# Output projection and feed-forward of the first 384 tokens moved between the recurrence stages of blocks 3 to 7

## The chip, the core and the metric

The kernel runs on one core of a Trainium2 chip. Its time is device microseconds from launch to end, the median of three runs. The engines are TensorE (PE), VectorE (DVE), ScalarE (ACT), GpSimd (POOL) and SyncE (SP, which here only issues the weight loads). Each has its own queue, executed in order; they meet through semaphores.

## What is computed

One step of a hybrid decoder layer, for 1024 prompt tokens and 8 sample tokens (1032 columns, kept with features on the partitions), model width 1024:

```python
h = rmsnorm(x, g_norm1) * (1 + sc1) + sh1
mix, states = token_mix(h, ...)       # h @ w_in, then HGRN2 | Mamba-2 | RWKV-7, then @ w_out
x = x + g1 * mix
h = rmsnorm(x, g_norm2) * (1 + sc2) + sh2
ff = (silu(h @ w_gate) * (h @ w_up)) @ w_down      # D_FF = 2816
x = x + g2 * ff
y = rmsnorm(x, g_final)
```

`sh1` to `g2` come from a modulation matmul of the conditioning vectors with `w_ada`. The recurrences carry a state over the tokens, so a token's mixed row needs all tokens before it; projection and feed-forward are independent from token to token.

## The kernel before

**Dense matmuls.** A dense product is cut into units (128 output features) and each unit into quanta, one for each chunk of 344 columns (`CH`, three chunks). In a quantum, `dense(q)` runs over the 128-row tiles k of the contraction: every fp32 product is made of three matmuls, hi by hi, lo by hi, hi by lo (lines 1067 to 1069). A unit's weights are loaded once by SP into one of three buffers (`RAW`, line 759), cast to `WHI` by ACT (`split_hi`, line 1547), and `WLO`, the remainder, is subtracted by DVE (`split_lo`, line 1944) or POOL (`split_rest`, line 846). Each quantum fills one PSUM bank, which ACT or DVE takes up (`bring_out`). The next quantum in that bank waits for that.

**Phases.** All engines follow written-out lists, with a barrier (`end_phase`) between them. PLAN1 holds the input projection, the last part of it in gaps of the WKV recurrence. PLAN2 holds the HGRN2 and Mamba-2 recurrences in eight blocks of 128 tokens. A block is the sequence hg_att, hg_state, mb_decay, hg_o, hg_logits, mb_prod, hg_sq, hg_gate, mb_turn, mb_sq, hg_out, hg_levels, mb_out, hg_x, where logits, gate, turn and levels are those of the next block. The main chain is: PE turns and attention matmuls (1015, 1348), state (1355), decay sums (1406), DVE's segments (2548), ACT's exponential (1851), DVE's product MM (2553), PE's products (1417, 1418, states 1421), then DVE's output and square (HT, 2504), the norms (1374, 1431), and for the next block DVE's differences and levels (2453 to 2470). hg_x turns one block of input tokens into `XT`, the residual. Sixteen quanta of the modulation matmul (`ada`, 1074) are dealt out, one each after mb_decay, mb_prod and mb_turn; each reads two `RAW` buffers. At the end of PLAN2 stand the samples' one-token updates (`smp_tok`, `smp_state`, `smp_out`; DVE lines 2587 to 2606), which pass through DRAM.

**PLAN3** is the rest: the mixed rows are split in hi and lo (`mixsplit`), then `out`, then the norm for each chunk (`sum`, `scaled`, `rest`: sum over partitions on PE at 1090, DVE, ACT at 1621, DVE), then gate and up (interleaved by chunk), with SiLU on ACT and the product on DVE, and `down` in four groups of 6, 6, 5 and 5 tiles, the last norm (`normed`), and nine turned output tiles (`y`) of which two buffers (`OT`) are written to DRAM in turn.

Of the kernel before, what the change touches and what calls it, by code (L numbers as in the profile page):

```python
# [33 lines left out]
F32 = mybir.dt.float32  # L34
# [19 lines left out]
GROUPS = [6, 6, 5, 5]  # L54
MAXG = max(GROUPS)
# [63 lines left out]
def dense_plan():  # L119
# [7 lines left out]
    units += [('out', t) for t in range(8)]  # L127
    f = 0
    for g, n in enumerate(GROUPS):
        for i in range(n):  # L130
            units += [('gate', f), ('up', f)]
            f += 1
        units += [('down', (g, d)) for d in range(KT)]
    return units, n1


def kernel_program(nc, ins, outs):
# [15 lines left out]
    UNITS, N1 = dense_plan()  # L153
    QUANTA, FIRSTQ, LASTQ = [], {}, {}
    u = 0
    while u < len(UNITS):
# [9 lines left out]
        elif kind == 'gate' or UNITS[u] in (('out', KT - 2), ('down', (len(GROUPS) - 1, KT - 2))):  # L166

            FIRSTQ[u + 1] = len(QUANTA) + 1
            for c in range(NCH):
                QUANTA += [(u, c), (u + 1, c)]  # L170
            LASTQ[u] = len(QUANTA) - 2
            LASTQ[u + 1] = len(QUANTA) - 1
            u += 2
            continue
        else:
            QUANTA += [(u, c) for c in range(NCH)]
# [5 lines left out]
    QP2 = LASTQ[N1 - 1] + 1  # L182
    NRAW, NSPL1, NSPL3 = 3, 2, 4
# [26 lines left out]
    SQUARED = [q for q, (u, _) in enumerate(QUANTA)  # L210
               if UNITS[u][0] == 'out' or (UNITS[u][0] == 'down' and UNITS[u][1][0] == len(GROUPS) - 1)]
    TILE_IN_GROUP = [i for n in GROUPS for i in range(n)]

    ctx = ExitStack()
    with ctx:
# [131 lines left out]
        HB2 = [r2.t(f"HB{i}", [P, 6, BLK]) for i in range(2)]  # L347
# [6 lines left out]
        HD = r2.t("HD", [P, 6, 2, BLK])  # L354
# [7 lines left out]
        HVD = r2.t("HVD", [P, 2, 4, BLK])  # L362
        HSH = r2.t("HSH", [P, 5, 2, 64])
        HO = r2.t("HO", [P, 2, BLK])
        HT = r2.t("HT", [P, 2, BLK])
        HR = r2.t("HR", [P, 2, BLK])
        XD = r2.t("XD", [P, 8, 64])
# [6 lines left out]
        CE = r2.t("CE", [P, 4, P])  # L374
        STt = r2.t("STt", [P, 4, 64])
# [13 lines left out]
        AEX = r2.t("AEX", [P, 8])  # L389
        r2b = Region(mix_end, hi)  # L390
        XT = r2b.t("XT", [P, KT, T])
        XTOK2 = [r2b.t(f"XTOK2_{i}", [P, D]) for i in range(2)]
        SHG = r2b.t("SHG", [P, 1024])
        SHT2 = r2b.t("SHT2", [P, 1024])
        STMP = Region(r2b.at - 4 * 2048, r2b.at).t("STMP", [P, 2048])
        SMT = r2b.t("SMT", [P, 2048])
        xb_at = r2b.at
        SSM = r2b.t("SSM", [P, 2048])
        STK = r2b.t("STK", [NS, 1024])
        r2b.t("XPAD", [P, 3 * T - 3072])  # L400

        xr1, xr2 = Region(h_end, mix_end - 4 * KT * T), Region(xb_at, r2b.at)
        XB = [(xr1 if t < 3 else xr2).t(f"XB{t}", [P, T]) for t in range(6)]
# [7 lines left out]
        stoken_at = r2b.at  # L411
        STOKEN = r2b.t("STOKEN", [NS, 768])
        ADT2 = Region(stoken_at, r2b.at).t("ADT2", [P, 512])

        r3 = Region(h_at, h_end)
        MHI = r3.t("MHI", [P, KT, T], F32R)
        MLO = r3.t("MLO", [P, KT, T], F32R)
        r3c = Region(h_at, h_end)
        H2I = r3c.t("H2I", [P, KT, T], F32R)
        H2L = r3c.t("H2L", [P, KT, T], F32R)  # L420
        xt_end = Region(mix_end, hi).at + 4 * KT * T
        r3b = Region(xt_end, hi)
        WHI3 = WHI1 + [r3b.t(f"WHI3_{i}", [P, KT, P], F32R) for i in range(NSPL3 - NSPL1)]
        WLO3 = WLO1 + [r3b.t(f"WLO3_{i}", [P, KT, P], F32R) for i in range(NSPL3 - NSPL1)]
# [2293 lines left out]
```

## Time and profile before

| | us |
|---|---|
| median of three runs (2036.17 to 2037.88) | 2037.71 |
| the profiled execution | 2036.94 |
| its span, first to last instruction | 2035.2 |
| PE busy in the span | 1704.0 (84%) |
| DVE busy | 871.1 (43%) |
| ACT busy | 490.7 (24%) |
| POOL busy | 164.9 (8%) |

Busy time of PE is the sum of matmul durations, and matmuls overlap, so a busy PE need not be at its peak. PEclk in the page is the granted clock of TensorE, in tenths of full speed. Its two levels here are 2.4 GHz (1.00) and 1.2 GHz (0.50), and a value between them is a mean over a stretch. In the page's slices, of 51 us each, the last digit of a row may stand for the kernel's end.

### The profile page before, as it was taken

The page shows a single profiled execution, that of the slowest core. Times are in us where ns is not written, and L with a number is a line of the kernel's source. Part 1 is how long each engine was busy: PE and PEld are TensorE (multiplying, and loading weights), DVE is VectorE, ACT ScalarE, POOL GpSimd, SP SyncE. Part 2 cuts the span into 40 slices and gives each one's busy share as a digit, 9 for nine tenths or more (in the row PEclk, how much of TensorE's full clock was granted, in tenths as well). Part 3 has the DMA queues.
Part 4 walks back from the last instruction along what each step waited for, and adds up shares of the span by engine and source line. Part 5 has one row for each costly group of instructions (what it writes and reads, how often), then busy time and mean ns, then how long its engine had stood idle before and what let it go on. Part 6 is the DMA issues. An engine that isn't in the chain of part 4 may idle for free.

```text
span 2035.2 us, 31284 instructions
## 1 busy us (share of the span) xinstructions
PE 1704.0 (84%) x13471; PEld 1535.2 (75%) x13471; DVE 871.1 (43%) x1989; ACT 490.7 (24%) x913; POOL 164.9 (8%) x286
## 2 busy tenths in 40 slices
PE   4898887888876738887774796999999999999996
PEld 2898777777764635444452796999999999999995
DVE  6305456663343545546554446223322332242245
ACT  3224222222221432222221324211121112111122
POOL 3501001110000221000102000000000000000000
PEclk9999888988877765666655898999999999999998
DMA  7111011100100232323201120111211121021002
GB/s 292 47 42 31 12 32 43 38 26 29 36 5 1 63 124 89 102 81 106 67 13 39 63 63 20 54 32 42 62 52 33 42 63 44 21 76 54 20 27 84
DMA packets 121633, 110.37 MB, mean 54 GB/s; under 512 B 4848, under 2 KB 109793, under 8 KB 120217
## 3 DMA queue, kind: packets, MB, share of 16 engines
q1 hardware_dynamic: 111106, 81.87, 13.1%
q0 software_dynamic: 7440, 23.27, 3.4%
q10 hardware_dynamic: 2950, 3.24, 0.4%
q8 instruction: 106, 1.74, 0.3%
q14 instruction: 31, 0.25, 0.0%
HBM read 95.23 MB, written 13.18 MB: 53 GB/s over the span
## 4 chain that ended last, share of the span: by engine, by line
PE 70%; DVE 18%; ACT 6%; issue 2%; DMA 2%; POOL 0%; SPq 0%; POOLq 0%; DVEq 0%; ACTq 0%
PE bank L1067 17%; PE bank L1069 17%; PE bank L1068 17%; PE bank L1015 2%; PE bank L1417 2%; PE bank L1418 2%; PE bank L1240 1%; PE bank L1241 1%; PE bank L1189 1%; PE bank L1406 1%; PE bank L1251 1%; PE bank L1196 1%; PE bank L1348 1%; PE bank L1431 1%; PE bank L1198 1%
## 5 line engine op out<-in xcount | busy, mean ns | idle before, releaser
L1067 PE MATMUL bank<-H2I,WHI 128*128 128x344 f32 x1056 | 339.3, 321 | 6.7 <-DVE H2L L2051 4.8
L1069 PE MATMUL bank<-H2I,WLO 128*128 128x344 f32 x1056 | 338.0, 320 | 0.0
L1068 PE MATMUL bank<-H2L,WHI 128*128 128x344 f32 x1056 | 338.0, 320 | 0.0
L1067 PE MATMUL bank<-HHI,WHI 128*128 128x344 f32 x624 | 213.4, 342 | 18.2 <-ACT STG L1579 7.0
L1068 PE MATMUL bank<-HLO,WHI 128*128 128x344 f32 x624 | 205.8, 330 | 0.0
L1069 PE MATMUL bank<-HHI,WLO 128*128 128x344 f32 x624 | 205.3, 329 | 0.0
L1067 PEld LDWEIGHTS bank<-H2I,WHI 128*128 128x128 f32 x1056 | 199.5, 189 | 7.5 <-issue 7.5
L1068 PEld LDWEIGHTS bank<-H2L,WHI 128*128 128x128 f32 x1056 | 199.1, 189 | 0.2 <-issue 0.2
L1069 PEld LDWEIGHTS bank<-H2I,WLO 128*128 128x128 f32 x1056 | 199.3, 189 | 0.0
L1067 PE MATMUL bank<-GHI,WHI 128*128 128x344 f32 x528 | 169.2, 320 | 0.0
L1068 PE MATMUL bank<-GLO,WHI 128*128 128x344 f32 x528 | 168.9, 320 | 0.0
L1069 PE MATMUL bank<-GHI,WLO 128*128 128x344 f32 x528 | 168.7, 320 | 0.0
L1944 DVE TENSOR_TENSOR WLO<-RAW,WHI 128x1024 fp32r<-128x1024 f32 (+2 forms) x93 | 102.8, 1110 | 151.7 <-ACT WHI L1547 151.5
L1547 ACT CAST WHI<-RAW 128x1024 fp32r<-128x1024 f32 (+2 forms) x110 | 105.8, 966 | 198.1 <-PE bank L1069 196.3
L1992 DVE TENSOR_TENSOR GU<-SGF,bank 128x344 f32<-128x344 f32 x66 | 33.8, 512 | 265.9 <-PE bank L1069 265.9
L1067 PEld LDWEIGHTS bank<-HHI,WHI 128*128 128x128 f32 x624 | 123.6, 198 | 22.0 <-ACT STG L1579 7.5
L2001 DVE SCALAR_TENSOR_TENSOR XT<-bank,MOD,XT 128x344 f32<-128x344 f32 (+1 forms) x120 | 68.6, 573 | 136.8 <-PE bank L1069 135.4
L1068 PEld LDWEIGHTS bank<-HLO,WHI 128*128 128x128 f32 x624 | 123.4, 198 | 0.7
L1069 PEld LDWEIGHTS bank<-HHI,WLO 128*128 128x128 f32 x624 | 122.9, 197 | 0.0
L1067 PEld LDWEIGHTS bank<-GHI,WHI 128*128 128x128 f32 x528 | 99.5, 189 | 0.1
L1068 PEld LDWEIGHTS bank<-GLO,WHI 128*128 128x128 f32 x528 | 99.2, 188 | 0.1
L1069 PEld LDWEIGHTS bank<-GHI,WLO 128*128 128x128 f32 x528 | 99.3, 188 | 0.0
(468 smaller groups left out, 2663.0 us busy)
## 6 DMA issues: line engine op xcount, KB each, us to landing
RAW<-in_w_ada SPq DMA_DIRECT2D x32, 512.0 KB, 4.3
RAW<-in_w_in SPq DMA_DIRECT2D x26, 512.0 KB, 3.8
RAW<-in_w_gate SPq DMA_DIRECT2D x22, 512.0 KB, 3.8
RAW<-in_w_up SPq DMA_DIRECT2D x22, 512.0 KB, 3.8
ADAW<-in_w_ada SPq DMA_DIRECT2D x8, 1024.0 KB, 19.3
RAW<-in_w_down SPq DMA_DIRECT2D x16, 384.0 KB, 3.4
RAW<-in_w_down SPq DMA_DIRECT2D x16, 320.0 KB, 3.1
XTOK<-in_x_prompt SPq DMA_DIRECT2D x8, 512.0 KB, 8.1
```

Source lines behind the costliest of these rows:

```text
L1015: return nc.tensor.transpose(out, in_, ident[0:n, 0:n])
L1067: mm(bank[:, 0:CH], whi[:, k, :], hi_[:, k, cols], start=(k == 0), stop=False)
L1068: mm(bank[:, 0:CH], whi[:, k, :], lo_[:, k, cols], start=False, stop=False)
L1069: last = mm(bank[:, 0:CH], wlo[:, k, :], hi_[:, k, cols], start=False, stop=(k == nk - 1))
L1189: last = mm(B0[HP[hp], jc * 64:jc * 64 + 64], AM[HP[hp], hp, jc, 64 * hp:64 * hp + 64], X[HP[hp], jc, :], start=True, stop=True)
L1196: mm(B1[HP[hp], jc * 64:jc * 64 + 64], Y[HP[hp], jc, :], PS[HP[hp], jc, :], start=True, stop=True)
L1417: mm(out, XD[:, h, :], MM[:, h, :], start=True, stop=False)
L1418: last = mm(out, STt[HP[gr], h % 4, :], CE[HP[gr], h % 4, :], start=False, stop=True)
L1547: a.copy(w_split(i)[0][:, 0:nk, :], RAW[u % NRAW][:, 0:nk, :]).then_inc(w_hi, 1)
L1944: v.tensor_tensor(wlo[:, 0:nk, :], RAW[u % NRAW][:, 0:nk, :], whi[:, 0:nk, :].bitcast(F32), ALU.subtract).then_inc(w_lo, 1)
L1992: v.tensor_tensor(GU[i % 2][:, :], SGF[i % 2][:, :], bank[:, 0:CH], ALU.mult).then_inc(evac['dve'], 1)
L2001: v.scalar_tensor_tensor(XT[:, t, c0:c0 + n], bank[:, 0:n], MOD[:, m + t, 0:1], XT[:, t, c0:c0 + n], ALU.mult, ALU.add).then_inc(evac['dve ...
```

## The change

Columns are now cut in chunks of 384, 320 and 328, and the units of projection and feed-forward stand twice in the list: part 0 has chunk 0 only (with down in six groups of 4, 4, 4, 4, 3 and 3 tiles), part 1 has chunks 1 and 2 (groups of 6, 6, 5, 5). Every weight tile of these products is so loaded and split twice.

Part 0 is put in PLAN2. A quantum with eight k tiles is issued in two halves of 12 matmuls, one of a down unit whole (12 or 9 matmuls). `FILL` says how many follow each stage in blocks 3 to 7: 20 a block, 16 in the last, which has no next block; 42 stand between the samples' steps, the last token turns and a barrier in two parts (`mark`, `join`), and 14 behind it. Part 0 uses PSUM banks 2 and 3 and two weight slots, so the HGRN2 stages give up banks 2 and 3: the second half of the attention goes to bank 0 and waits for ACT's copies, and hg_state waits for DVE's masking. POOL makes the remainders of weights up to the samples' part, DVE from there. SiLU of part 0 is made of Exp, Ln and Exp on ACT with a clamp and a product on DVE, because the loaded table set has no Silu. The token turns of blocks 3 to 8 move behind block 7. All modulation quanta move to blocks 0 to 2, six a block. The first three output tiles are turned and written at the beginning of PLAN3.

```diff
+GROUPS = [[4, 4, 4, 4, 3, 3], [6, 6, 5, 5]]
+FC0 = [0, 384, 704]
+FCW = [384, 320, 328]
...
-            b = 3 if q < QP2 else q % 7
+            b = 3 if q < QP2 else 2 + (q - QP2) % 2 if q < QP2A else q % 7
...
-            s = i % NSPL1 if i < n1s else (i - n1s) % NSPL3
+            s = i % NSPL1 if i < n1s else (i - n1s) % NSPL1 if i < n2s else (i - n2s) % NSPL3
...
+        ffn = [('mixsplit', 0), ('split', n1s)]
+        for q in range(QP2, QP2A):
+            ffn += [('split', i) for i in splits_at.get(q, [])]
+            if unit_k(UNITS_OF(q)) == KT:
+                ffn += [('half', (q, 0)), ('half', (q, 1))]
+            else:
+                ffn.append(('half', (q, None)))
+            if q - 1 >= QP2 and q - 1 != LASTQ[N1 + 7]:
+                ffn.append(('ev', q - 1))
+            if q == LASTQ[N1 + 7]:
+                ffn += [('ev', q), ('sum', 3), ('scaled', 3), ('rest', 3)]
+        ffn.append(('ev', QP2A - 1))
+
+        def fill(n):
+
+            while ffn and n >= 0:
+                n -= ffn[0][0] == 'half'
+                if n >= 0:
+                    PLAN2.append(ffn.pop(0))
+
+        FILL = {'hg_att': 2, 'hg_state': 1, 'mb_decay': 3, 'hg_o': 2, 'mb_prod': 3, 'hg_sq': 2, 'mb_turn': 2, 'mb_sq': 2,
+                'hg_levels': 2, 'mb_out': 1}
         for b in range(NB):
...
-                if item[1] == NB:
+                if item[1] == NB or (item[0] == 'hg_x' and b > 2):
                     continue
                 PLAN2.append(item)
-                if item[0] in ('mb_decay', 'mb_prod', 'mb_turn') and late:
+                if b > 2:
+                    fill(FILL.get(item[0], 0))
+                elif item[0] in ('hg_att', 'mb_decay', 'hg_o', 'mb_prod', 'hg_sq', 'mb_turn') and late:
...
+        samples_at = len(PLAN2)
+        PLAN2.append(('smp_tok', 0))
+        fill(6)
+        PLAN2.append(('mix_final', 0))
+        fill(4)
+        PLAN2.append(('smp_state', 0))
+        fill(8)
+        PLAN2.append(('smp_out', 0))
+        fill(4)
+        for i in range(3, 9):
+            PLAN2.append(('x', i))
+            fill(2)
+        PLAN2.append(('mark', 0))
+        fill(8)
+        PLAN2 += [('join', 0), ('mixsplit', 1), ('mixsplit', 2)]
+        fill(len(ffn))
+        PLAN2 += ffn
...
+        early = [('sum', 6), ('normed', 6)] + [('ya', (i, h)) for i in range(3) for h in range(2)]
...
+        for at, (what, arg) in enumerate(PLAN2 + PLAN3):
+            if what == 'split':
+                LO_BY[arg] = 'pool' if at < samples_at else 'dve'
...
                     for hp, bank in ((0, H1), (1, H0)):
+                        if hp:
+                            pe.wait_ge(*A('turned'))
...
                 elif stage == 'state':
                     pe.wait_ge(*A('v'))
+                    pe.wait_ge(*V('masked'))
...
+            def gate_scale(q):
+
+                n = GATES.index(q)
+                act.wait_ge(evac['dve'], EVN[q])
+                link(a.activation(SGF[n % 2][:, :], GU[n % 2][:, :], ACT.Exp, scale=-1.0))
+                link(a.activation(SGF[n % 2][:, :], SGF[n % 2][:, :], ACT.Ln, bias=1.0))
+                a.activation(SGF[n % 2][:, :], SGF[n % 2][:, :], ACT.Exp, scale=-1.0).then_inc(ga_sig, 1)
...
+                    if c == 0:
+                        dve.wait_ge(ga_sig, i + 1)
+                        link(v.tensor_tensor(GU[i % 2][:, 0:w], GU[i % 2][:, 0:w], SGF[i % 2][:, 0:w], ALU.mult))
+                        dve.wait_ge(dense_done, q + 1)
+                        v.tensor_tensor(GU[i % 2][:, 0:w], GU[i % 2][:, 0:w], bank[:, 0:w], ALU.mult).then_inc(
+                            evac['dve'], 1)
```

## Rows read from the trace of the kernel before

**Rows 1.** The page: the granted clock in 40 slices of the span.

```profile
PEclk9999888988877765666655898999999999999998
```

**Rows 2.** Windows: length, busy of PE, PEld, DVE, ACT, POOL, clock, DMA share, GB/s.

```profile
765.00:890.00 125.00, 101.42 (x1045) 60.90 (x1045) 69.86 (x230) 31.36 (x61) 11.28 (x12) 0.59 0.28 94
890.00:1087.00 197.00, 147.89 (x1662) 93.57 (x1662) 106.86 (x347) 48.04 (x95) 17.91 (x19) 0.61 0.19 58
1087.00:1136.00 49.00, 10.72 (x47) 7.02 (x48) 26.71 (x38) 12.29 (x21) 14.03 (x23) 0.50 0.18 63
...
1230.00:1266.00 36.00, 17.88 (x98) 16.87 (x98) 22.86 (x53) 14.22 (x27) 0.00 (x0) 0.81 0.00 0
1266.00:2008.00 742.00, 737.88 (x4674) 737.18 (x4675) 225.26 (x400) 138.59 (x232) 0.00 (x0) 1.00 0.15 44
2008.00:2036.00 28.00, 11.37 (x62) 9.24 (x60) 12.34 (x25) 6.10 (x11) 4.81 (x9) 0.72 0.39 151
1300.00:1400.00 100.00, 100.00 (x638) 100.00 (x637) 23.44 (x38) 18.79 (x34) 0.00 (x0) 1.00 0.12 35
```

**Rows 3.** Timeline (start us, us, engine, line, operation): first dense matmuls of PLAN3.

```profile
1136.26 0.49 PE L1068 MATMUL bank<-MLO,WHI 128*128 128x344 f32 x1
1136.55 0.49 PE L1069 MATMUL bank<-MHI,WLO 128*128 128x344 f32 x1
```

**Rows 4.** Timeline of block 4 and the next block's start.

```profile
929.24 0.41 PE L1015 MATMUL bank<-ident,HB 128*128 128x128 f32 x2 [1.20 <-DVE XT L2009]
...
937.10 2.52 PE L1406 MATMUL bank<-triu,DTA 128*128 128x128 f32 x16
...
944.32 1.29 DVE L2553 TENSOR_TENSOR MM<-SEG,CBM 128x512 f32<-128x512 f32 x2 [1.12 <-ACT SEG L1851]
...
945.67 0.69 PE L1417 MATMUL bank<-MM,XD 128*64 128x128 f32 x2 [1.96 <-DVE MM L2553]
...
955.54 1.12 PE L1421 MATMUL bank<-XDE,BT 128*64 128x256 f32 x4
...
970.53 0.41 PE L1015 MATMUL bank<-ident,HB 128*128 128x128 f32 x2 [1.36 <-DVE XT L2009]
```

**Rows 5.** Lines from 1130 us on: groups of instructions, count, busy, mean ns.

```profile
L1944 DVE TENSOR_TENSOR WLO<-RAW,WHI 128x1024 fp32r<-128x1024 f32 x52 | 63.2, 1223 | 64.2 <-ACT WHI L1547 64.2
...
L1547 ACT CAST WHI<-RAW 128x1024 fp32r<-128x1024 f32 x52 | 54.0, 1043 | 84.4 <-PE bank L1069 84.4
...
L1621 ACT ACTIVATE H2I<-H,MOD 128x344 fp32r<-128x344 f32 x16 | 7.8, 569 | 0.0
```

**Rows 6.** DMA issues, 765 to 1090 us: count, size, median us to landing.

```profile
RAW<-in_w_ada SPq DMA_DIRECT2D x29, 512.0 KB, 4.7
```

**Rows 7.** Timeline of DVE and POOL around POOL's splits, before 710 us.

```profile
170.17 2.60 DVE L2242 TENSOR_TENSOR BK<-KP,ENB 64x256 f32<-64x256 f32 x1
...
230.81 0.41 DVE L2238 TENSOR_TENSOR AR<-MX,EB 64x256 f32<-64x256 f32 x1
...
232.22 2.56 POOL L846 TENSOR_TENSOR WLO<-RAW,WHI 128x1024 fp32r<-128x1024 f32 x1 [31.63 <-ACT WHI L1547]
232.45 2.62 DVE L2238 TENSOR_TENSOR AR<-MX,EB 64x256 f32<-64x256 f32 x1
...
705.68 2.04 DVE L2331 TENSOR_TENSOR SWK<-SWK,SWV 128x1024 f32<-128x1024 f32 x1
```

**Rows 8.** Chain that ended last, 480 to 670 us: one step of each WKV block.

```profile
494.56 1.22 PE bank L1251 x2
...
559.46 1.23 PE bank L1251 x2
...
614.33 1.23 PE bank L1251 x2
...
662.06 1.23 PE bank L1251 x2
```

**Rows 9.** PE's waits between 1087 and 1136 us: for whom, us, times, longest.

```profile
PE bank L1453 <- DVE SO L2592: 10.4, 1, 10.4
```

More of the change, by code:

```diff
@@ L126, in dense_plan @@
     n1 = len(units)
[L127 to L134, printed above, removed]
+    ends = []
+    for part, groups in enumerate(GROUPS):
+        units += [('out', t) for t in range(8)]
+        f = 0
+        for g, n in enumerate(groups):
+            for i in range(n):
+                units += [('gate', f), ('up', f)]
+                f += 1
+            units += [('down', (part, g, d)) for d in range(KT)]
+        ends.append(len(units))
+    return units, n1, ends[0]
 def kernel_program(nc, ins, outs):
@@ L165, in kernel_program @@
             continue
-        elif kind == 'gate' or UNITS[u] in (('out', KT - 2), ('down', (len(GROUPS) - 1, KT - 2))):
+        elif kind == 'gate' or (u >= N2 and (UNITS[u] == ('out', KT - 2) or (last_group(u) and
+                                                                             UNITS[u][1][2] == KT - 2))):
             FIRSTQ[u + 1] = len(QUANTA) + 1
-            for c in range(NCH):
+            for c in chunks(u):
                 QUANTA += [(u, c), (u + 1, c)]
@@ L175, in kernel_program @@
         else:
-            QUANTA += [(u, c) for c in range(NCH)]
+            QUANTA += [(u, c) for c in chunks(u)]
         LASTQ[u] = len(QUANTA) - 1
@@ L714, in kernel_program @@
                     PLAN2.append(('mm', late.pop(0)))
+                    if not late:
+                        PLAN2.append(('adt', 2))
         assert not late
-        PLAN2 += [('adt', 2), ('smp_tok', 0), ('hg_x', NB), ('mix_final', 0), ('smp_state', 0), ('smp_out', 0)]
-        PLAN3 = [('mixsplit', 0)]
-        PLAN3 += [('split', i) for i, u in enumerate(SPLIT)
-                  if u >= N1 and any(i in splits_at[q] for q in splits_at if q < QP2)]
-        PLAN3 += [('mixsplit', c) for c in range(1, NCH)]
@@ L1040, in dense @@
                 bank = BK8[BANK[q]]
-                if PREV[q] is not None:
+                if PREV[q] is not None and half != 1:
                     pe.wait_ge(evac[evac_engine(PREV[q])], EVN[PREV[q]])
@@ L1049, in dense @@
                     return
-                if c == 0:
+                if c == chunks(u)[0] and half != 1:
                     pe.wait_ge(w_hi, SIDX[u] + 1)
@@ L1483, in _ @@
                     ada_turn(arg)
-                elif what == 'ev':
-                    pass
+                elif what == 'half':
+                    dense(*arg)
+                elif what == 'sum':
+                    chunk_sum(arg)
+                elif what == 'x':
+                    pe.wait_ge(hs_dve, HS_DVE.index('out') + 1)
+                    turn_x(9 + arg, XTOK3)
                 elif what[:3] == 'hg_':
@@ new lines, in ffn_step @@
+            def ffn_step(what, arg):
+                if what == 'split':
+                    split_hi(arg)
+                elif what == 'ev':
+                    bring_out(arg)
+                    if arg in GATES and QUANTA[arg][1] == 0:
+                        gate_scale(arg)
+                    if arg in UPS:
+                        gu_head(UPS.index(arg))
+                    if arg in SQUARED:
+                        tile_squares(arg)
+                elif what == 'mixsplit':
+                    hi_, _, cols = hcols(arg)
+                    a.copy(hi_[:, :, cols], MIX[:, :, FC0[arg]:FC0[arg] + FCW[arg]]).then_inc(mix_hi, 1)
+                elif what == 'sum':
+                    norm_scale(arg)
+                    if arg == 5:
+                        tables(SILU_SET)
+                elif what == 'rest':
+                    head(arg)
```

572 lines of the change are left out of this document (334 added, 238 removed).

## The prediction, made before the changed kernel was run

> **What bounds the kernel now.** I read the page first: TensorE (PE) is busy over most of the span, and its granted clock [rows 1] is full at the start and from slice 23 on, but between 0.5 and 0.7 in the middle. Then the same by stage, with the stretches cut at the kernel's own marks [rows 2]. In 1136 to 2008 us (output projection and feed-forward) PE is busy without a gap, bar the norm between them (1230 to 1266). In 765 to 1087 us (the eight recurrence blocks) all four engines are partly idle and the clock is 0.6; the 49 us after it (samples' states and the splitting of the mixed rows) hold 10.7 us of PE work. A dense matmul of 344 columns starts every 157 ns at full clock (638 in 100 us, [rows 2]) and every 0.29 us at the lower level, 1.2 GHz [rows 3]. A block follows a chain over PE, DVE and ACT and takes 41.3 us, from one set of turns (929.24) to the next (970.53) [rows 4]; its largest piece is 11.0 us of PE work at the low clock, 945.67 to 956.66.
>
> So the change moves PE-bound work into a stretch where PE waits. The whole question is how much of the moved work is hidden there.
>
> **Term 1, what leaves the end.** Chunk 0 is 384 of 1032 columns. The number of dense matmuls is unchanged (5328: 576 in the projection, 4752 behind it), and so are the columns, so at full clock their cost is the same: 5328 x 0.157 = 835 us, of which chunk 0 is 384/1032, 311 us (one matmul of 384 columns 0.175 us, a half of 12 of them 2.1 us). Against it stand six half turns of finished rows that now lie between dense quanta, some 1 us. The norm between projection and feed-forward stays: for two chunks instead of three the idle of PE comes out about as before (two chains of ACT, DVE and the second chunk's, 8 operations of 0.49 us each [rows 5]), bounds -5 to +5. Term 1 = -310, bounds -303 to -315. Splitting hi and lo of every weight a second time costs nothing in this stretch: a unit now has 7.1 us of PE work for 1.04 us on ACT and 1.22 us on DVE [rows 5].
>
> **Term 2, the end.** Three of nine output tiles are written before it. The last stretch is 28 us [rows 2], of which the last chunk's norm takes 10 and seven tiles the rest, 2.6 us for each. Four are left; but the norm hid part of the first: -5 instead of -8, bounds -9 to 0.
>
> **Term 3, blocks 0 to 2 (765 to 890 us).** Sixteen modulation quanta stand six to a block instead of three. Each reads two weight tiles of three buffers, and a tile lands 4.7 us after its issue [rows 6]; so two quanta closer than some 5 us make PE wait. Walking the order: the quantum behind hg_att delays the decay matmuls by 2 us (these start the chain to MM), the one behind hg_o waits for its tile and delays mb_prod by 3.8, the two behind hg_sq and mb_turn bring it to 9. That is 9 + 9, and block 2 with four quanta and one more turn 6: +24, bounds +8 to +32 (the low one if the clock rises with the added work).
>
> **Term 4, blocks 3 to 7 (890 to 1087, 197 us).** The fills are 20 halves a block, 16 in the last: 96 halves, 42 us of PE a block. PE's own work of a block is 16.7 us at full clock: turns and att 3.0, state 1.0, decay 1.8 (2.52 traced, mostly at full clock [rows 4]), o 2.4, products and states 6.1 (11.0 traced low), sums and turns 2.4. Rows 4 has the largest of them, the rest is read from the same timeline. Token turns and modulation are gone from these blocks. So nothing can be below 59 us. I walked one block with the engines' queues in the order of the plan. Where it stalls is in mb_decay: from the end of the decay matmuls to the end of MM pass 6.0 us (939.6 to 945.6, [rows 4]), and DVE, in order, can't take up the finished quantum's bank before. The half-filled quantum ends 2.1 us in, the next one needs that bank (there are two), so PE waits 4.6 us. Elsewhere fills of 4 to 6 us cover the chain (the 10 us from HT to the next block's factors lie beside 9 halves), and weights arrive 0.4 to 0.9 us ahead: 1.04 on ACT and 2.4 on POOL against 4.2 us of PE for a unit. That gives 64 us.
>
> Two costs come on top. POOL's split of 128x1024 holds DVE: one operation of DVE took 2.62 us beside it instead of 0.41 [rows 7], and so at twelve of the seventeen splits that the trace has, from 170.17 to 705.68; at the other five DVE had nothing to read from SBUF. There will be ten a block. In the walk DVE's lateness reaches PE at hg_sq and at two banks, at most 6.5 us; I take 3, since POOL and DVE often miss each other. The Trainium skill, page "SBUF — State Buffer", section "SBUF: two separate sides", says that DVE and GpSimd take a shared port pair as an exclusive lock for a whole instruction, when DVE has two SBUF inputs or a two-port mode; by that rule, the trace agrees, and all 6.5 us would be due: a block of 72.5, and 2042 us. The clock: dense work holds it at 1.00 in 1300 to 1400, but with PE's waits between 1230 and 1266 it was 0.81, and among small matmuls here 0.61 [rows 2]. PE's stalls and small matmuls will lower it at times: 0 to 6 us a block, I take 2. A block is 69, bounds 60 to 80.
>
> From another side: before 700 us, dense quanta (7 of 24 matmuls, 26.4 us) lie between WKV stages, and such a block takes 64.9 us, the last one without them 47.7 [rows 8]: 65% of the added work showed. By that ratio a block here, 36 us without modulation and turns, comes to 36 + 0.65 x 42 = 63; by the same 9 us hidden, to 69.
>
> One-offs: the last block has four halves less (-9); in block 3 the first half waits for the split of the mixed rows on ACT, then DVE (+7); behind the 16th projection half, squares, sum, scale, ACT's head and DVE's rest follow one another with nothing on PE (three times 8 operations of 0.49 us at 344 columns [rows 5] and more at 384, 17.6 us with squares and sums, and a low clock after it: +20); at each group's turn to down 2.2 us (+6); down units are split almost as fast as they are used (+3). 5 x 69 + 27 = 372 against 197: +175, bounds +130 to +230.
>
> **Term 5, from block 7 to the rest (1087 to 1136, 49 us).** Here lie 56 halves or down units. Before the join: 84 us dense, 10.5 us own, and waits that stay. PE reaches smp_state before DVE has the state sums (it waited 10.4 us there [rows 9]; now 4.5), then runs one quantum ahead while DVE does 10 us on SSM (7.3), the start and smp_out 7, clock 5, two turns to down 4.4: 123. After it 25 us dense, and 5 for the other chunks' splits and one turn. 153 against 49: +104, bounds +85 to +125.
>
> **Sum.** -310 - 5 + 24 + 175 + 104 = -12. The profiled execution took 2036.94 (span 2035.2), 0.8 below the median of the runs. So I predict 2025 us. A block of 71.4 us instead of 69 eats the whole gain: this is a forecast close to the edge.
>
> **Rivals.** (A) PE is all that counts. The clock stays full in the blocks, POOL's splits fall where DVE reads PSUM, and PE's queue runs well ahead: a block is 64, the tail's waits halve (-10), the modulation quanta cost +14. 2025 - 25 - 10 - 10 = 1980. For it: rows 8's ratio (63); at 1300 to 1400 dense work keeps the clock at 1.00. Against it: rows 7. (B) Slower: DVE is held by POOL's splits. Every one of the ten a block delays HT, the diffs and levels or a bank's release, PE waits for each, stands 12 us a block and loses its clock to that. A block is 76: +35, 2060. It decides from 71.4 us a block on. For it: rows 7, and that the chain of a block hangs on DVE [rows 4]. Against it: nine halves stand beside that chain. It is what the lock of the Trainium skill (named above) makes of this plan when no split is lucky; rows 7 agree with the lock, not yet with the price. (C) What is hidden and what is added cancel within a block or two: 2034 to 2042, no change (0.2%, 4 us, is about what a measurement of this kernel can tell from none). (D) The change doesn't reach its place: modulation or x loads hold block 3 up, or the second reading of the weights is late. It is 38.8 MB more in some 500 us, 78 GB/s on top of 58, where the last stretch carried 151 [rows 2]; it would be a part of B.
>
> **Chances.** Forecast (blocks of 66 to 71 us, 2005 to 2033) 0.33; A and beyond 0.23; C 0.07; B, with D 0.37. So faster 0.56, same 0.07, slower 0.37. Range: from all bounds of A with some to spare, 1970, to B with a block of 80 us, 2078. The likeliest's own range is 2005 to 2033.
>
> **What would show it.** The turns' starts (L1015, HB) in blocks 3 to 7: 69 us apart, and PE's granted clock there 0.85 to 0.95. PE's wait for DVE behind the decay matmuls 4 to 5 us; a gap of 17 us once in block 3. DVE operations of 2 us and more beside POOL's split in these blocks. Blocks 0 and 1 of 50 us. From the join to the end some 590 us, with PE at full clock. The forecast is wrong if blocks lie under 64 or over 72 us, or if the stretch behind the join is not 310 us shorter.

## The result and the profile after

The changed kernel takes 2073.0 us (median of 4 runs, 2070.9 to 2082.8), the kernel before 2037.8 on the same chip: a ratio of 1.0184, 95% interval 1.0156 to 1.0211. It is slower, where faster was forecast. The profiled execution took 2070.9 us, its span is 2069.2. The page's lines that answer to [rows 1] (busy time, and the granted clock in 40 slices):

```profile
PE 1685.7 (81%) x13471; PEld 1527.3 (74%) x13471; DVE 963.5 (47%) x2087; ACT 592.1 (29%) x1057; POOL 289.0 (14%) x348
PEclk9999888988866866759799899889998999999998
```

The low stretch is shorter than before, and yet the time is longer. So the next view is the windows by stage, cut at the turns that open a block, at the samples' turns and at the first dense matmul of chunks 1 and 2. First the kernel before, in the same cuts, then the changed one. Columns: window, its length, busy time (instructions) of PE, PEld, DVE, ACT, POOL, granted clock, DMA share, GB/s.

```profile
765.00:890.30 125.30, 101.44 (x1046) 60.95 (x1046) 70.00 (x230) 31.36 (x61) 11.28 (x12) 0.60 0.28 95
890.30:1091.00 200.70, 148.99 (x1666) 94.24 (x1666) 108.43 (x352) 49.84 (x100) 19.04 (x21) 0.61 0.19 60
1091.00:1135.80 44.80, 9.44 (x42) 6.11 (x42) 24.81 (x31) 10.29 (x15) 12.90 (x21) 0.50 0.16 54
1135.80:2035.20 899.40, 860.96 (x5412) 856.30 (x5412) 304.40 (x551) 184.50 (x312) 4.81 (x9) 0.98 0.16 47
```

```profile
765.00:902.50 137.50, 102.89 (x1106) 55.59 (x1106) 70.53 (x231) 32.07 (x62) 10.16 (x10) 0.67 0.42 136
902.50:1006.10 103.60, 67.64 (x558) 60.50 (x559) 53.39 (x110) 33.85 (x52) 29.45 (x14) 0.80 0.19 55
1006.10:1083.20 77.10, 65.85 (x557) 58.89 (x556) 38.21 (x97) 26.93 (x46) 26.81 (x17) 0.91 0.25 74
1083.20:1159.00 75.80, 64.92 (x556) 58.19 (x555) 40.03 (x95) 27.59 (x47) 27.78 (x16) 0.93 0.22 65
1159.00:1232.30 73.30, 64.45 (x558) 56.98 (x557) 39.72 (x93) 27.34 (x46) 29.46 (x15) 0.93 0.27 77
1232.30:1305.90 73.60, 53.93 (x500) 48.05 (x499) 29.04 (x63) 21.84 (x40) 26.11 (x17) 0.89 0.25 72
...
1305.90:1484.10 178.20, 136.81 (x706) 129.02 (x707) 92.83 (x137) 58.87 (x96) 17.14 (x29) 0.87 0.35 109
1484.10:2069.20 585.10, 545.92 (x3634) 542.45 (x3634) 235.64 (x437) 148.67 (x243) 4.81 (x9) 0.98 0.24 72
```

Read the lengths in pairs, and put the forecast beside them:

| stretch | before | after | difference | forecast |
|---|---|---|---|---|
| blocks 0 to 2 | 125.3 | 137.5 | +12 | +24 |
| blocks 3 to 7 | 200.7 | 403.4 | +203 | +175 |
| block 7 to chunk 1's first matmul | 44.8 | 178.2 | +133 | +104 |
| from there to the end | 899.4 | 585.1 | -314 | -315 |
| sum | | | +34 | -12 |

The stretch that the work left came out to the microsecond. The two that took it up are 28 and 29 us over. (The forecast cut them at 1087 and not at 1091 us; against its own lengths, 372 and 153 us, they are 31 and 25 over.) In blocks 3 to 7 lie 1152 of the moved matmuls, 201.6 us at 0.175, and the time grew by 203; behind block 7 lie 624, 109 us, and it grew by 133. On balance the stretches grew by as much as the moved matmuls take at full clock, and more.

What PE waits for in blocks 3 to 7 (columns: who waited for whom, us in all, times, longest):

```profile
PE bank L1183 <- DVE XTA L2191: 20.7, 6, 5.4
PE bank L1183 <- DVE HAL L2235: 16.4, 1, 16.4
PE bank L1183 <- DVE MIXR L2246: 11.8, 3, 6.0
PE bank L1183 <- DVE HAL L2295: 10.8, 1, 10.8
PE bank L1183 <- DVE GU L2166: 8.5, 2, 4.3
PE bank L1122 <- ACT HK L2045: 6.0, 1, 6.0
```

All but the last are waits of dense matmuls, which the kernel before did not have here. XTA and GU L2166 are finished quanta whose bank DVE has not taken up, MIXR L2246 is the turn to the down units, HAL L2235 the norm, HAL L2295 the split of the mixed rows. One of them is shown close up, in block 4, behind the decay matmuls. PE (start, length, engine, line, output and input, and in brackets the idle time before it and what ended that):

```profile
1020.22 0.34 PE L1185 MATMUL bank<-HAH,WLO 128*128 128x384 f32 x1
1024.83 0.69 PE L1183 MATMUL bank<-HAH,WHI 128*128 128x384 f32 x1 [4.27 <-DVE GU L2166]
1025.32 0.53 PE L1184 MATMUL bank<-HAL,WHI 128*128 128x384 f32 x1
...
1030.05 0.34 PE L1184 MATMUL bank<-HAL,WHI 128*128 128x384 f32 x1
1030.23 0.33 PE L1185 MATMUL bank<-HAH,WLO 128*128 128x384 f32 x1
```

and DVE beside it:

```profile
1019.73 2.16 DVE L2790 TENSOR_SCALAR SEG<-bank,ACOL 128x128 f32<-128x128 f32 x8 [2.62 <-ACT E L2029]
1023.01 1.29 DVE L2795 TENSOR_TENSOR MM<-SEG,CBM 128x512 f32<-128x512 f32 x2 [1.12 <-ACT SEG L2033]
1024.23 0.55 DVE L2166 TENSOR_SCALAR GU<-bank 128x384 f32<-128x384 f32 x1
```

DVE stands in its decay stage, waits in it twice for ACT, and only then reads the bank. PE waits 4.27 us. Behind the wait the starts lie 0.32 us apart (384 columns at 1.2 GHz) up to 1029.80, and 0.175 again after that (2.4 GHz): 16 slow matmuls, 2.3 us. **A wait of 4 us costs 6 to 7.**

### The profile page after: what moved, and what is told of

It is laid out like the page before. It is cut to its first block, busy times and chain, and to the rows that moved or that the text cites. A ratio compares the mean times of both kernels' runs of the same rounds, so it can differ in the third digit from the quotient of the medians.

```text
span 2069.2 us, 31916 instructions
## 1 busy us (share of the span) xinstructions
PE 1685.7 (81%) x13471; PEld 1527.3 (74%) x13471; DVE 963.5 (47%) x2087; ACT 592.1 (29%) x1057; POOL 289.0 (14%) x348
## 4 chain that ended last, share of the span: by engine, by line
PE 67%; DVE 19%; ACT 6%; DMA 4%; issue 3%; POOL 0%; SPq 0%; POOLq 0%; DVEq 0%; ACTq 0%
PE bank L1183 17%; PE bank L1184 16%; PE bank L1185 16%; PE bank L1122 2%; DMA RAW<-in_w_ada 2%; PE bank L1191 1%; PE bank L1551 1%; PE bank L1552 1%; PE bank L1370 1%; PE bank L1371 1%; PE bank L1319 1%; ACT WHI L1690 1%; PE bank L1381 1%; PE bank L1326 1%; PE bank L1328 1%
## 5 line engine op out<-in xcount | busy, mean ns | idle before, releaser
L1690 ACT CAST WHI<-RAW 128x1024 fp32r<-128x1024 f32 (+4 forms) x210 | 187.9, 897 | 346.7 <-PE bank L1185 343.1
L1183 PE MATMUL bank<-HBH,WHI 128*128 128x328 f32 (+1 forms) x832 | 261.1, 314 | 14.3 <-DVE HBL L2235 10.1
L1184 PE MATMUL bank<-HBL,WHI 128*128 128x328 f32 (+1 forms) x832 | 259.6, 312 | 0.0
L1185 PE MATMUL bank<-HBH,WLO 128*128 128x328 f32 (+1 forms) x832 | 258.8, 311 | 0.0
L944 POOL TENSOR_TENSOR WLO<-RAW,WHI 128x1024 fp32r<-128x1024 f32 (+1 forms) x79 | 165.7, 2099 | 512.0 <-ACT WHI L1690 512.0
L1183 PE MATMUL bank<-HAH,WHI 128*128 128x384 f32 x416 | 151.8, 365 | 56.6 <-DVE HAL L2235 16.4
L1183 PEld LDWEIGHTS bank<-HBH,WHI 128*128 128x128 f32 x832 | 157.1, 189 | 15.5 <-issue 15.3
L1185 PEld LDWEIGHTS bank<-HBH,WLO 128*128 128x128 f32 x832 | 157.4, 189 | 0.0
L1184 PEld LDWEIGHTS bank<-HBL,WHI 128*128 128x128 f32 x832 | 157.1, 189 | 0.2
L1184 PE MATMUL bank<-HAL,WHI 128*128 128x384 f32 x416 | 146.1, 351 | 0.0
```

The costliest lines, as they stand in the source:

```text
L944: g.tensor_tensor(wlo[:, 0:nk, :], RAW[u % NRAW][:, 0:nk, :], whi[:, 0:nk, :].bitcast(F32), ALU.subtract).then_inc(w_lo, 1)
L1183: mm(bank[:, 0:w], whi[:, k, :], hi_k, start=(k == 0), stop=False)
L1184: mm(bank[:, 0:w], whi[:, k, :], lo_k, start=False, stop=False)
L1185: last = mm(bank[:, 0:w], wlo[:, k, :], hi_k, start=False, stop=(k == nk - 1))
L1690: a.copy(w_split(i)[0][:, 0:nk, :], RAW[u % NRAW][:, 0:nk, :]).then_inc(w_hi, 1)
```

## The experiments

Nearly every edit is in the plan, the list of stages and quanta that all engines follow, and the matmuls of the reference's work are the same in all. A half is one of the two pieces of 12 matmuls that a quantum is issued in. The code shown is cut to what bears on the edit. Ratios are to the kernel before on the same chip; the changed kernel's is 1.0184.

**e1**, the bank taken up between the halves of the next quantum:

```
-  ffn += [('half', (q, 0)), ('half', (q, 1))] ... then ('ev', q - 1)
+  ffn += [('half', (q, 0)), ('ev', q - 1), ('half', (q, 1))]
```

> In part 0 a finished quantum's bank is taken up between the two halves of the next quantum and not behind both, so DVE does it before it waits in mb_decay. Theory S (the order of DVE's queue makes PE wait, and each wait is followed by low-clock matmuls): the five waits behind the decay matmuls (4.33, 4.27, 4.3, 4.33, 5.40 us, 22.6 in all) go, and with them the slow halves behind them (24 matmuls in 6.80 instead of 4.45 us, about 11 in all): 2073 - 30 = 2043, blocks 4 to 6 of 70 us. Rival L (DVE is late because POOL's splits hold it, so the same lateness shows at the next bank): -5 to -10, 2065, blocks of 75.

It measured 1.0191 (1.0165 to 1.0216): no gain, neither theory's number. The waits behind the decay matmuls did go in blocks 3 to 5 and stayed in 6 and 7 (4.3 and 5.4), where the quanta are down units, which the edit gives no middle. In their place PE waits ahead of the mamba block's sum of squares, here in block 5 (PE, then ACT):

```profile
1150.23 2.07 PE L1564 MATMUL bank<-T,ones 128*128 128x128 f32 x8 [5.19 <-ACT T L2035]
```

```profile
1147.52 0.60 ACT L1689 CAST WHI<-RAW 128x512 fp32r<-128x512 f32 x1
...
1149.13 0.52 ACT L1745 ACTIVATE SGF<-SGF 128x384 f32<-128x384 f32 x1
1149.56 0.61 ACT L2035 ACTIVATE T<-YS 128x512 f32<-128x512 f32 x1
```

The squares T stand behind part 0's weight and gate instructions on ACT, though YS had been ready for 19 us (DVE wrote it until 1130.6). In blocks 3 to 7 PE waits for T 16.1 us at four places, in the changed kernel 1.3 at one. The wait had moved, not gone.

**e2**, the low parts by DVE in all blocks (`LO_BY[arg] = 'dve'`):

> The low parts of part 0's weights in blocks 3 to 7 are made by DVE (1.23 us for 128x1024 as measured) instead of POOL (2.1 to 2.4 us). Rival L (POOL's splits hold DVE, rival B of the prediction): the hold goes, 35 us faster, 2038. Theory S (the hold is hit seldom; in block 4 it lengthened DVE's instructions by 1.5, 1.1 and 0.5 us): DVE has ten more instructions a block, each behind ACT's high part and that behind PE's release of the slot, in the middle of the recurrence's chain: 0 to +20 us, 2073 to 2093.

1.0357 (1.0328 to 1.0387), blocks 4 to 6 of 90, 90 and 84 us: 35 us slower than the change, above both theories. PE waits 107.0 us in blocks 3 to 7 instead of 86.6. The run does not price the lock by itself, for it takes the hold away and at the same time puts some ten more instructions a block into DVE's queue. In the changed kernel 17 instructions of DVE in blocks 3 to 7 lie more than 0.3 us over the median of their line and shape in these blocks, by 25.1 us in all, 14 of them by over 1 us, each beside a split of POOL; in e2 there is one, by 0.5 us. One of them, with POOL's split beside it (DVE, then POOL):

```profile
1028.20 2.05 DVE L2246 TENSOR_TENSOR MIXR<-GU,MIXR 128x384 fp32r<-128x384 f32 x1 [0.58 <-ACT MIXR L1785]
```

```profile
1027.45 2.38 POOL L944 TENSOR_TENSOR WLO<-RAW,WHI 128x1024 fp32r<-128x1024 f32 x1 [6.40 <-ACT WHI L1690]
```

So the hold is real, and no wait of PE stands behind this one. Others do stand ahead of a wait, in blocks 3 and 7 (DVE; undisturbed, the four copies take 0.91 us in block 7, and the product MM took 1.29 in block 4 above):

```profile
910.32 4.61 DVE L2729 COPY HAD<-HAT 32x128 f32<-32x128 f32 x4
...
1259.68 2.36 DVE L2795 TENSOR_TENSOR MM<-SEG,CBM 128x512 f32<-128x512 f32 x2 [1.12 <-ACT SEG L2033]
```

Behind the first comes PE's wait of 10.8 us for the mixed rows, behind the second the one of 5.4. In e2, without POOL's splits, these two are 8.2 and 4.3, and the norm's is 14.3 instead of 16.4. So some 6 us of the hold reach PE in blocks 3 to 7, of the 28 that these blocks are over the forecast.

**e3**, nothing between the stages; the 96 halves in one piece behind block 7:

```
-  if b > 2:
-      fill(FILL.get(item[0], 0))
+  if b > 2:
+      pass
...
+  fill(96)          # behind block 7
```

> Nothing of part 0 is put between the stages of blocks 3 to 7; the 96 halves run in one piece behind block 7, all else as in the changed kernel. It prices what the interleaving hides. Theory S (waits and low clock eat what is hidden): blocks alone 36 us (41.3 without modulation and turns), five 180, 96 halves at 2.1 us 202, the norm's wait and the turns to down with their slow matmuls 30: 412 us where the changed kernel takes 403, so 2075 to 2085. Rival H (interleaving hides 9 us and more of each block's waits, the loss is elsewhere): 2073 + 45 and more, 2118.

1.0415 (1.0396 to 1.0435), 2125 us: by the ratios the interleaving does hide 47 us, by the windows (449.5 against 403.4 us) 46. Theory S was wrong here. One thing more differs than was meant: which engine makes the low parts goes by the place in the plan, so those of the 96 halves are made by DVE (POOL is busy 4.1 us in the second line below). The same holds for the halves that e11 and e17 put behind block 7. These runs price the place and the engine together. Windows of a block alone, and of block 7 with the 96 halves behind it:

```profile
947.10:985.00 37.90, 27.09 (x316) 17.83 (x316) 22.62 (x75) 9.79 (x20) 3.19 (x3) 0.59 0.04 11
...
1063.50:1356.90 293.40, 241.46 (x1461) 226.86 (x1462) 139.22 (x224) 101.69 (x155) 4.07 (x6) 0.86 0.33 97
```

A block alone takes 39.0 (mean of four), not the 36 that the prediction has without modulation and turns; before, the same four blocks took 40.2. But the 39.0 hold a wait of the change's own: hg_state now waits for DVE's masking, because the stages gave up two banks, 1.2 us a block which the kernel before does not have. PE's wait for it in e3's blocks 3 to 6:

```profile
PE bank L1490 <- DVE HAS L2718: 4.8, 4, 1.2
```

So the modulation and the turns had cost between 1.2 and 2.4 us a block, not 5. And 96 halves in one piece take 254 us, 2.65 for each and not 2.1, with the norm, the turns to down and their slow matmuls in them. So the part's own chains, not only the recurrence's, make PE wait.

**e4**, the first gate unit of the next group ahead of this group's down units:

```
   for g, n in enumerate(groups):
       for i in range(n):
-          units += [('gate', f), ('up', f)]
+          if part or i or not g:
+              units.append(('gate', f))
+          units.append(('up', f))
           f += 1
+      if not part and g + 1 < len(groups):
+          units.append(('gate', f))
       units += [('down', (part, g, d)) for d in range(KT)]
```

> In part 0 the first gate unit of the next group runs before the down units of this group, so that the last up's product is split while PE works. Theory S: five turns to down (2.87, 2.87, 6.02, 3.77, 3.26 us of PE's wait, 18.8 in all, and some 8 us of slow matmuls behind them) go, the sixth stays: 2073 - 25 = 2048. Rival L (DVE is late by more than one unit's 4.2 us there): half of it, 2062.

1.0101 (1.0081 to 1.0122), 17 us less than the change; between the two. Of the five waits four went and one was 2.0 us; the sixth stayed. The wait of 8.1 us for XTA behind the samples' mamba state is one of 7.4 for GU here, and XTA's waits in blocks 3 to 7 rose from 20.7 to 28.7 us.

**e5**, e1 and the mamba sum of squares right behind the HGRN one:

```
-  ('hg_sq', b), ('hg_gate', b + 1), ('mb_turn', b + 1), ('mb_sq', b), ...
+  ('hg_sq', b), ('mb_sq', b), ('hg_gate', b + 1), ('mb_turn', b + 1), ...
```

> e1 (banks taken up between the halves) and, besides, the mamba block's squares and their sum stand right behind the HGRN squares, ahead of the next block's gates and turns. In e1 the waits behind the decay matmuls went in two of five blocks and 2.9 to 4.6 us more came up ahead of the sum of squares, where ACT's squares queued behind a gate quantum's three instructions (PE waited for T in all 19.6 us at five places). Theory M (a wait removed at one stage comes up at the next one that is queued behind part 0's work on ACT or DVE; this is the next one): those waits go as well, 12 to 20 us less than e1: 1.011 of the kernel before, 2060. Rival C (the chain of the recurrence itself, 39 us alone, with the halves between its stages sets the block): the time moves to another stage, 1.017 to 1.020.

1.0144 (1.0126 to 1.0162): 10 us less than e1, where M had 12 to 20.

**e6**, e4, the bank right behind each quantum's last half, and e5's move:

> e4 (first gate of the next group ahead of the down units), the bank of every quantum is taken up right behind its last half, down units too, and the sum of squares is moved as in e5. Theory M: e4's 1.010, less the decay waits of blocks 3 to 7 (22 us with the slow matmuls behind them some 30) less what comes up elsewhere: 0.995 to 1.003, 2035. Rival C: 1.008 to 1.012. Rival O: DVE now waits in its queue for each quantum's end and the recurrence's instructions stand behind it: slower than e4, 1.015.

1.0158 (1.0126 to 1.019): rival O's number, but not its cause. PE's waits in its blocks 3 to 7:

```profile
PE bank L1186 <- POOL WLO L947: 29.1, 15, 4.7
...
PE bank L1186 <- DVE XTA L2194: 6.6, 2, 3.3
```

Banks come late twice instead of ten times, and the weights fifteen times: ACT now does the bank's gate instructions first, then the high part, and POOL's 2.4 us start behind that.

**e10**, e4 and e5's move, with the order weights, bank, half:

```
   ffn += [('split', i) for i in splits_at.get(q, [])]
+  if q - 1 >= QP2 and q - 1 != LASTQ[N1 + 7]:
+      ffn.append(('ev', q - 1))
...
   ffn += [('half', (q, 0)), ('half', (q, 1))]
```

> e4 with the sum of squares moved, and on ACT and DVE the next unit's weights stand ahead of the finished quantum's bank, both ahead of the next half. In e6 (bank first) the waits for DVE's banks went, and waits for the low parts that POOL makes came in their place (15 of them, 1.4 to 4.8 us, some 30 us). Theory M (the order of what is queued decides, and here neither is late): waits in blocks 4 to 6 of 5 us instead of 10, a block of 68 to 70, 15 to 20 us less than e4: 1.000 to 1.003. Rival C (two banks, two weight slots and the recurrence's chain leave no order without a wait): waits of 8 to 12 us a block again, blocks of 73 to 76, 1.009 to 1.013.

1.0036 (1.0018 to 1.0053). That is 13 us less than e4, near theory M's 15 to 20. PE waits 69.0 us in blocks 3 to 7, where the changed kernel has 86.6. The waits in its blocks, and block 4:

```profile
PE bank L1187 <- POOL WLO L948: 9.0, 4, 4.4
PE bank L1187 <- DVE XTA L2195: 6.6, 2, 3.3
```

```profile
1011.70:1078.50 66.80, 60.90 (x557) 54.83 (x556) 45.28 (x95) 27.81 (x48) 26.68 (x16) 0.97 0.25 74
```

It does the 557 instructions of the changed kernel's block 4 in 66.8 us instead of 77.1: the wait is 5.9 instead of 11.2, and PE's busy time is 60.9 instead of 65.9, for the clock is 0.97 and not 0.91. DVE was held more than before (27 instructions, 35.5 us over the medians in blocks 3 to 7, counted as in e2), and the kernel is faster all the same.

**e19**, e10 without e4's edit:

> The changed kernel with the next unit's weights and the finished bank ahead of the next half on ACT and DVE, and the sum of squares moved, the first gate unit of a group behind the down units as in the change. Theory M (the turn to down and the queues' order are separate losses): e10's 1.0036 plus e4's gain of 0.0083: 1.011 to 1.013, 2063. Rival N (with the queues in order the last up's product is split in time anyway): 1.005.

1.0096 (1.0077 to 1.0115), nearer to M. The queues' order (with the sum of squares moved) gives 0.009 and the turn to down 0.008 by themselves, 0.015 together: nearly additive.

**e7**, e4, and behind block 7 the samples' states earlier and in pieces (the plan before and after, in short):

```
-  fill(6), ('mix_final', 0), fill(4), ('smp_state', 0), fill(8), ('smp_out', 0)
+  fill(6), ('mix_final', 0), ('smp_hg', 0), fill(4), ('smp_state', 0),
+  ('smp_ssm', 0), fill(2), ... ('smp_ssm', 3), fill(2), ('smp_out', 0)
```

> e4, and behind block 7 the samples' HGRN state is computed by DVE four halves before PE's sum over it, and the mamba state's instructions (10.6 us in one piece) in four pieces with two halves between. Theory S: PE's waits of 8.3 us (for SO) and 8.1 us (behind the mamba state) go, with some 6 us of slow matmuls behind them: 20 us less than e4, 1.000 of the kernel before. Rival D (DVE has no room there: 16 us of state work beside banks and low parts): 8 us less, 1.006.

1.013 (1.0115 to 1.0146): no gain. **e8**, e4 with the norm beside block 4's first stages:

> e4, and the norm between part 0's projection and its first gate unit runs beside block 4's attention, state and decay stages: seven halves (four of block 3, three of block 4) move behind block 7. PE's wait of 16.4 us there covered nothing. Theory S: the 6 us of PE's own work and the turns of block 4 go into it, and the chain of block 4 starts some 10 us sooner: 8 to 12 us less than e4, 1.005. Rival C: ACT and DVE do 16 us of norm in the middle of the recurrence's chain, and the seven halves (14.7 us) are missing as cover: no gain, 1.010 to 1.014.

1.0156 (1.0123 to 1.0189). Blocks 3 to 7 came to 387 us instead of 400, and the stretch behind them, with seven halves more, from 167.5 to 183.9. **e12**, e10 with both:

> e10, with e7's order of the samples' states and e8's place of the norm. Theory M: the norm's place saved 12.6 us in blocks 3 and 4 (e8) against seven halves more behind block 7 (14.7 us there), and e7's order nothing by its time; with banks and weights in time both gain: 5 to 10 us less than e10. Rival C: within 3 us of e10.

1.0061 (1.0042 to 1.008): no gain over e10 (the intervals overlap), but the stretch behind block 7 did 708 matmuls in 172.1 us where e10 does 624 in 171.6. Hence **e14**, e10 with e7's order alone:

> e10 with e7's order behind block 7 (the samples' HGRN state on DVE four halves ahead of PE's sum, the mamba state in four pieces). Theory T (with banks and weights taken up in time, DVE's long piece is what PE waits for there): e12's tail took 172.1 us for 708 dense matmuls, e10's 171.6 for 624; 14.7 us less than e10, 0.997 of the kernel before. Rival D (e12's gain came from the halves that stood there, not from the order; as in e7 nothing is gained): within 3 us of e10, 1.003.

0.9975 (0.996 to 0.9989), that stretch 162.1 us. What brought nothing on e4 brings 0.006 here; why it needs e10's order was not told apart.

**e13**, the changed kernel with 80 matmuls of 128x128, whose result nobody reads, behind the sum of squares in block 3:

> The changed kernel with 80 small matmuls (128x128, their result is not read) issued behind the sum of the first 384 tokens' squares, where PE waits 16.4 us for the norm: no other work is added or moved. If the slow matmuls that follow a wait come from the wait, the dense matmuls behind this one start every 0.175 us at once instead of 0.29 for the first ones: 48 of them in 8.5 us instead of 9.9, and block 3 is 1.5 to 3 us shorter. If the low clock has another cause there (the recurrence's small matmuls), they stay as slow.

There is one execution of it, so its time decides nothing; the trace does. The dense matmuls behind the norm, in the changed kernel and in e13, there with the small matmuls ahead of them (160 records for the 80):

```profile
996.33 0.66 PE L1183 MATMUL bank<-HAH,WHI 128*128 128x384 f32 x1 [16.37 <-DVE HAL L2235]
...
997.11 0.52 PE L1185 MATMUL bank<-HAH,WLO 128*128 128x384 f32 x1
```

```profile
990.10 18.03 PE L1212 MATMUL bank<-ones,ident 128*128 128x128 f32 x160
1007.88 0.42 PE L1183 MATMUL bank<-HAH,WHI 128*128 128x384 f32 x1
...
1008.31 0.34 PE L1185 MATMUL bank<-HAH,WLO 128*128 128x384 f32 x1
```

With PE busy in between they are fast at once. The wait makes the slow matmuls. The Trainium skill, page "TensorE: Matmul & The Clock Gate", section "HAM oscillation — how this bites in real kernels", says that waits between bursts of matmuls make each burst start slow again; this pair agrees. Their number here was 9, not some 24 (1.3 us), and block 3 was 103.4 instead of 103.6 us; the dummies ran some 1.2 us past the norm.

**e11**, e10 with some ten halves a block, 50 more behind block 7:

> e10 with 46 halves in blocks 3 to 7 instead of 96; the other 50 run in one piece behind block 7. A half behind block 7 costs 2.65 us (254 us for 96 in e3), and interleaving all 96 saved 46 us against that. Rival L (hiding is in proportion to the halves): half of it is lost, e10 + 23 us. Theory F (the first halves between two stages go into waits and lift the clock, the later ones only make the chain longer): blocks of 47 to 50 us, and the time within 8 us of e10, on either side.

1.0067 (1.0048 to 1.0086), 6 us over e10, within the 8 that theory F allowed; its blocks of 47 to 50 us did not come (blocks 3 to 6 are 60.9, 62.1, 51.5 and 51.0). In these four blocks e10's 40 halves more take 82.6 us more (308.1 against 225.5), 2.07 for each: the second ten hide nothing. They pay only by what a half costs behind block 7: with block 7 and what stands behind it, as far as the samples' turns, it is 376 us in e10 and 383 in e11.

**e15**, e14 with three modulation quanta ahead of block 0; **e16**, e15 with PE's turns of the samples' tokens two halves later and three halves between the splits of chunks 1 and 2; **e17**, e16 with 14 halves a block:

> e14, and three of the sixteen modulation quanta run ahead of block 0, where PE waits 23 us for the decays' inputs. Theory Q (blocks 0 to 2 are longer because quanta stand closer than their weights land): three waits of 2 us and three quanta of 1.9 us leave these blocks: 6 to 10 us less than e14. Rival K (they take cover from the chain's own waits, as before in six blocks): 0 to 3 us less.

> e15, PE's turns of the samples' tokens two halves later (PE waited 5.4 us for ACT there) and three halves between the splits of the two other chunks' mixed rows (PE waited 6 us there). Theory M (each wait and the slow matmuls behind it go): 12 to 15 us less than e15. Rival C (they come up again behind the next stage): 0 to 4 us less.

> e16 with 14 halves a block (12 less in all behind block 7's two missing stages: some 28 halves more run in one piece behind block 7). Theory F (the last halves of a block hide nothing, and they lengthen the chain): within 4 us of e16, on either side. Rival L (each half that leaves a block costs what e3 lost for each, 0.5 us): 10 to 15 us more than e16.

0.9992 (0.9976 to 1.0008), 0.996 (0.9945 to 0.9975) and 1.0062 (1.0041 to 1.0082). The quanta's place brings nothing: e15 lies 3 us above e14, outside both theories. e16 gains 6.5 us, between its theories. e17 is some 20 us worse than e16, over both theories. Its blocks 3 to 6 take 275.9 us and e16's 309.2, so the 24 halves gone from them save 1.4 us each, and all behind these blocks takes 56 us longer, 2.3 for each. Against e11's 225.6 its 16 halves more cost 3.1 each. Its block 4 has 28.5 us of waits in 81.7, 15.2 of them the norm, which has moved there from block 3, and 8.4 for DVE's factors ahead of the next block's turns. So neither "the last halves hide nothing" nor a price for each describes it; where the halves stand does, and which of its places is the bad one stays open.

**e18**, e16 with the quanta back:

> e16 with the modulation quanta back in blocks 0 to 2 as in the changed kernel. e15 stood 0.0017 over e14 (its three quanta ahead of block 0 started that block 5 us later in the profile and gained 0 to 3 us behind it), e16 0.0032 under e15. If both hold by themselves: 0.994 to 0.995 of the kernel before. Rival: the placing of the quanta does nothing at all, 0.996 as e16.

**0.9929 (0.9907 to 0.995), 2026.6 us: 0.7% faster than the kernel before, and so faster than both.** Its blocks 3, 5 and 7 and the stretch behind:

```profile
906.20:1007.00 100.80, 65.57 (x557) 57.97 (x558) 58.28 (x111) 33.88 (x52) 29.64 (x14) 0.79 0.19 57
...
1073.80:1145.70 71.90, 63.74 (x557) 57.30 (x556) 44.71 (x97) 27.88 (x47) 27.61 (x15) 0.94 0.27 79
...
1214.30:1282.30 68.00, 58.98 (x522) 52.68 (x522) 35.57 (x70) 23.40 (x43) 26.78 (x19) 0.92 0.26 75
1282.30:1437.60 155.30, 127.82 (x683) 120.14 (x683) 90.97 (x134) 57.19 (x95) 16.01 (x27) 0.90 0.41 125
```

Blocks 3 to 7 take 376.1 us and that stretch 155.3, instead of 403.4 and 178.2; blocks 4 to 6 (66.8, 71.9, 68.6) are what was forecast, 69. The forecast's lengths, 372 and 153 us, are nearly those of this plan. (In it the samples' turns stand two halves later, so 4 us of matmuls count to block 7 and not to the stretch.)

## Why the prediction was wrong

- **Term 1 and term 2** (-315): measured -314.
- **Term 3** (+24): measured +12, within its bounds. The ten waits for modulation tiles are there (18.4 us in all), at most 2.4 each where 3.8 was priced once.
- **Term 4** failed. Of a block's 69 us the floor of 59 holds (42 dense and 17.3 of its own by the changed kernel's timeline): block 4 is 77.1, less 11.2 of waits and 59.3 leaves 6.6 for slow matmuls, and blocks 5 and 6 leave 5.6 and 5.2. The walk's stall in mb_decay, 4.6, was 4.3 in four blocks and 5.4 in the last (three times for XTA, twice for GU). The step that failed is "Elsewhere fills of 4 to 6 us cover the chain": 4 to 7 us of other waits a block are there, for the turn to down (2.9, 2.9, 6.0 where 2.2 was priced), for banks of down units (2.2, 3.1), for T and for the weights. The second is "0 to 6 us a block, I take 2" for the clock: 5 to 7 by this difference, 5.2, 5.1 and 3.3 by the 36, 35 and 23 dense matmuls that start 0.32 us apart, for these waits slow what follows. The last block, forecast at 60, was 73.6, with 13.7 us of waits in the block and 6.0 ahead of the samples' turns. Block 3 was 103.6 against 96 from its parts (69 + 20 + 7); the mixed rows' wait was 10.8 where 7 stood.
- **Term 5** failed in the same two ways: waits of 41.4 us (178.2 less 136.8 busy) against some 28, slow matmuls of 15 (136.8 less 109 dense and 13 of its own) against 5. smp_state was 8.3 where 4.5 was said, SSM 8.1 against 7.3. DVE's piece:

```profile
1345.28 1.29 DVE L2843 TENSOR_SCALAR SSM<-SSM,SV 128x2048 f32<-128x2048 f32 x1
...
1353.58 2.29 DVE L2848 TENSOR_REDUCE SY<-SMT 128x32 f32<-128x2048 f32 x1
1355.78 0.61 DVE L2191 SCALAR_TENSOR_TENSOR XTA<-bank,MOD,XTA 128x384 f32<-128x384 f32 x1
```

- **Rival B** had a block's length (76; measured 75.4 over blocks 4 to 6) by luck, for in the main it had not the cause: it laid the lateness to POOL's lock. The Trainium skill, page "SBUF — State Buffer", section "SBUF: two separate sides", is borne out by the lengthened instructions. But only some 6 us of the hold reach PE in blocks 3 to 7 (e2), and e10 is 30 us faster than the change with more of it. What the lock costs by itself, in the stages' own chain too, no run shows. The rival that should have stood beside it is the plain one: part 0's instructions and the recurrence's stand in one queue on each of ACT, DVE and POOL, with two banks and two weight slots, and each waits behind the other's dependencies. e4, e10, e19 and e14 take that back without touching the lock. Whether a third bank or weight slot would do the same was not tried.
- **The second side** ("36 us without modulation and turns") started from a block 3 us too short (39.0 in e3). By the same ratio it would have given 66, still far from 75. And the ratio came from one pair of steps: the step between them in [rows 8], with one quantum of 3.8 us, takes 54.9 us, 7.1 more than the one without, which is not 65%. The WKV blocks were no measure for this chain.
- **The splits of [rows 7]**: "at the other five DVE had nothing to read from SBUF" fits four of them. At the fifth (534.80) two DVE instructions read a mask in SBUF beside a bank, and were not held (0.45 us each).
- **The profile's signs**: turns 69 us apart was wrong (77.1, 75.9, 73.2), the clock of 0.85 to 0.95 right in blocks 4 to 7 (0.91, 0.93, 0.93, 0.89; block 3 had 0.80), the gap once in block 3 right (16.4), 4 to 5 us behind the decay matmuls right, blocks 0 and 1 of 50 us wrong (47.5 and 43.2), 590 us at the end: 585.1. The second reading of the weights (rival D) was never late: no wait of PE in blocks 3 to 7 names it.

What stays open: the waits of 16.4 and 10.3 us in block 3, which e8's move did not turn into time; why e14's order needs e10's; what the lock costs by itself; and e17.

## What to carry to other kernels

Work moved into an engine's idle time brings its own chain of the other engines with it. Walk that chain through every in-order queue that it shares, not only the first stall, and price each wait of some 4 us at one and a half times its length where the clock falls behind it. When one wait is removed and the time stays, look for the next instruction that stands in the same queue before calling the theory dead: e6 and e10 differ only in the order of two items, the finished bank and the next weights, and lie at 1.016 and 1.004. And price a hidden thing by the run that takes it out (e3), since what it had cost before may be little, and look in that run's plan for what else has moved.

## What the runs showed of the hardware

- Behind a wait of 4.27 us of PE 16 dense matmuls ran at half the clock, behind one of 16.37 us only 9; with matmuls in the wait, none. So the loss is not in proportion to the wait.
- A dense matmul of 384 columns starts every 0.32 us at 1.2 GHz and every 0.175 at 2.4.
- POOL's split of 128x1024 takes 2.4 us, DVE's 1.23; moving the work to the faster engine cost 35 us (e2), with 20 us more of PE's waits in blocks 3 to 7.
- Beside POOL's split single DVE instructions of 0.2 to 0.7 us took up to 2.5, 17 of them in the changed kernel's blocks 3 to 7. With the splits on DVE one was lengthened, by 0.5 us.
